# Products of probabilities and values of two attention stages, cut in quarters and placed behind the next heads' scores

## The reference

```
def gqa_attend(q, k, v, sink=None):
    ...
    s = jnp.einsum('bqhgd,bkhd->bhgqk', q.reshape(b, tq, hkv, g, d), k).astype(jnp.float32) * d ** -0.5
    ...
    o = jnp.einsum('bhgqk,bkhd->bqhgd', p.astype(v.dtype), v)
```

## Time and profile before

| | us |
|---|---|
| median of 3 runs | 4357.2 |
| lowest, highest | 4356.22, 4358.87 |
| profiled execution, its own time | 4357.44 |
| span of the profiled execution | 4355.6 |
| PE busy in the span | 3966.4 (91%) |
| DVE busy | 2239.5 (51%) |
| ACT busy | 781.6 (18%) |
| POOL busy | 1283.9 (29%) |
| mean granted TensorE clock | 0.934 of full |

### The profile page before, as it was taken

How to read it: one execution, slowest core, us unless ns; L and a number is a source line. 1 busy time by engine, 2 the same in 40 slices (tenths; PEclk the granted TensorE clock), 3 DMA queues, 4 the chain that set the end, 5 groups by cost and what they waited for, 6 DMA issues and landing times.

```text
span 4355.6 us, 45380 instructions
## 1 busy us (share of the span) xinstructions
PE 3966.4 (91%) x18926; PEld 3230.5 (74%) x18926; DVE 2239.5 (51%) x3645; ACT 781.6 (18%) x1462; POOL 1283.9 (29%) x522
## 2 busy tenths in 40 slices
PE   7976789999997889999999877999999999779998
PEld 5965459999985468888887745788788877457886
DVE  4824556876663462234347364733552473746334
ACT  3014432011122421100002222100100022221001
POOL 1310002333331034444443300444444433003443
PEclk9989899999998999999999956999999999569999
DMA  5410002344321012232222200222232222002222
GB/s 200 150 34 1 1 6 75 119 129 126 124 68 39 0 63 97 97 111 97 97 97 84 82 1 1 82 97 97 82 99 97 97 85 85 0 1 83 97 97 82
DMA packets 103695, 335.61 MB, mean 77 GB/s; under 512 B 11426, under 2 KB 11586, under 8 KB 103236
## 3 DMA queue, kind: packets, MB, share of 16 engines
q1 hardware_dynamic: 78192, 282.29, 19.4%
q10 hardware_dynamic: 25300, 50.43, 3.7%
HBM read 330.58 MB, written 2.10 MB: 76 GB/s over the span
## 4 chain that ended last, share of the span: by engine, by line
PE 59%; DVE 6%; ACT 2%; issue 1%; DVEq 0%; ACTq 0%
PE PS L497 50%; PE PS L979 1%; DVE XH L778 1%; PE PS L1861 1%; PE PS L499 0%; DVE H_r L655 0%; PE PS L1613 0%; PE PS L1614 0%; ACT arena L877 0%; PE PS L970 0%; PE PS L890 0%; PE PS L1864 0%; DVE small L1009 0%; PE PS L1631 0%; PE PS L2028 0%
## 5 line engine op out<-in xcount | busy, mean ns | idle before, releaser
L497 PE MATMUL PS<-arena_r,ring_hi 128*128 128x512 f32 (+1 forms) x6272 | 2120.4, 376 | 107.2 <-DVE H_r L655 102.3
L2220 POOL TENSOR_TENSOR ring_r<-ring,ring_hi 128x1024 fp32r<-128x1024 f32 x518 | 1283.7, 2479 | 3036.8 <-DVE ring_hi L337 3036.8
L497 PE MATMUL PS<-arena_r,ring_r 128*128 128x512 f32 (+1 forms) x4800 | 1800.9, 375 | 0.0
L497 PEld LDWEIGHTS PS<-arena_r,ring_hi 128*128 128x128 f32 x6272 | 1177.5, 189 | 291.5 <-issue 108.2
L497 PE MATMUL PS<-H_r,ring_hi 128*128 128x512 f32 (+1 forms) x3328 | 1249.9, 376 | 0.0
L497 PEld LDWEIGHTS PS<-arena_r,ring_r 128*128 128x128 f32 x4800 | 907.0, 189 | 132.9
L497 PEld LDWEIGHTS PS<-H_r,ring_hi 128*128 128x128 f32 x3328 | 632.4, 190 | 93.5 <-issue 0.5
L337 DVE CAST ring_hi<-ring 128x1024 fp32r<-128x1024 f32 x518 | 502.7, 973 | 276.1 <-DMA ring<-weights_dram 275.6
L1482 DVE SCALAR_TENSOR_TENSOR arena<-arena,PS 128x512 f32<-128x512 f32 x88 | 60.4, 687 | 447.3 <-PE PS L497 447.3
L1478 ACT ACTIVATE arena<-PS 128x512 f32<-128x512 f32 x88 | 52.6, 598 | 1073.5 <-PE PS L497 1073.5
L1093 DVE SCALAR_TENSOR_TENSOR XH<-PS,mods,XH 128x256 f32<-128x256 f32 (+1 forms) x144 | 68.5, 524 | 209.2 <-PE PS L497 209.2
(11 more groups left out here) (336 smaller groups left out, 3353.6 us busy)
## 6 DMA issues: line engine op xcount, KB each, us to landing
ring<-weights_dram SPq DMA_DIRECT2D x534, 512.0 KB, 3.3
rstd<-ada_later_dram ACTq DMA_DIRECT2D x54, 256.0 KB, 2.8
mean<-ada_later_dram ACTq DMA_DIRECT2D x53, 256.0 KB, 2.7
ada_extra<-ada_later_dram ACTq DMA_DIRECT2D x53, 256.0 KB, 2.8
XH<-xT_dram ACTq DMA_DIRECT2D x1, 3072.0 KB, 23.2
out_dram<-XH SPq DMA_DIRECT2D x8, 256.0 KB, 2.0
con<-second_dram ACTq DMA_DIRECT2D x1, 1536.0 KB
con<-first_dram ACTq DMA_DIRECT2D x1, 1280.0 KB, 7.9
```

The lines of the kernel that those rows point to most:

```text
L497: ins = pe.matmul(PS[:, o.bank, 0:hi - lo], w[:, 0, :], x, **flags)
L2220: nc.gpsimd.tensor_tensor(ring_lo[:, slot, :, :], ring[:, slot, :, :], ring_hi[:, slot, :, :].bitcast(F32), ALU.subtract).then_inc(lo_read ...
```

## The change

Only `attention` is edited, and so both stages. The block of L979 is cut in four quarters by key tiles: with 6 tiles 1, 2, 1, 2; with 5 tiles 1, 1, 1, 2; with 4 tiles one each; with 2 tiles 0, 1, 0, 1. Group g's quarters stand in steps 4g + 6 to 4g + 9, each behind that step's scores. The last group keeps its block, in the same step as before. The waits for `at_tc` and `at_oc` stand before the first quarter, and the copy-out on ACT moves from step 4g + 7 to 4g + 10. No instruction is added or taken away.

```
-                    if i >= 3 and (i - 3) % 4 == 3:
-                        gi, g = (i - 3) // 4, units[i - 3][0]
+                    if i >= 6:
+                        gi, quarter = (i - 6) // 4, (i - 6) % 4
+                        g = groups[gi]
                         kts = key_tiles(g)
-                        pe.wait_ge(at_tc.sem, at_tc.at("pe", i - 3))
-                        if gi >= 2:
-                            pe.wait_ge(at_oc.sem, at_oc.at("pe", gi - 2))
-                        for t, kt in enumerate(kts):
-                            ins = pe.matmul(PS[0:g["m"], 6 + gi % 2, :], g["v"](kt), turned[gi % 2][:, t, :],
+                        if quarter == 0:
+                            pe.wait_ge(at_tc.sem, at_tc.at("pe", 4 * gi + 3))
+                            if gi >= 2:
+                                pe.wait_ge(at_oc.sem, at_oc.at("pe", gi - 2))
+                        last = gi == len(groups) - 1
+                        for t in range(0 if last else len(kts) * quarter // 4, len(kts) if last else len(kts) * (quarter + 1) // 4):
+                            ins = pe.matmul(PS[0:g["m"], 6 + gi % 2, :], g["v"](kts[t]), turned[gi % 2][:, t, :],
                                             start=(t == 0), stop=(t == len(kts) - 1))
-                        ins.then_inc(at_o.sem, 1)
+                        if last or quarter == 3:
+                            ins.then_inc(at_o.sem, 1)
...
-                    if i >= 4 and (i - 4) % 4 == 3:
-                        gi, g = (i - 4) // 4, units[i - 4][0]
+                    if i == n + 3 or (i >= 10 and (i - 10) % 4 == 0):
+                        gi = len(groups) - 1 if i == n + 3 else (i - 10) // 4
+                        g = groups[gi]
                         act.wait_ge(at_o.sem, at_o.at("act", gi))
                         g["put"](PS[0:g["m"], 6 + gi % 2, :].rearrange("p (h q) -> p h q", h=4)).then_inc(at_oc.sem, 1)
```

## The result

Eight runs of the changed kernel gave 4310.8, 4314.9, 4315.5, 4339.1, 4339.2, 4339.6, 4340.4 and 4340.7 us: median 4339.2, against 4357.3 for the kernel before (4351.8 to 4359.4). The ratio is 0.9938, 95% interval 0.9914 to 0.9963: faster, clear of noise though by less than 1%, but not by a single amount. The times lie at **two levels** 25 us apart, and the profiled execution (4310.8) is one of the lower. Its mean granted clock is 0.935; that of the upper runs is 0.928. The forecast of 4314.3 fits the lower level, and the median lies outside the range of 4306 to 4329.

What follows compares the result with a forecast made beforehand. Bound by neither PE's work nor the DVE/ACT latency alone, paid one after the other in both attentions. Waits 21.4 + 18.7, less 2.7 block starts, plus 5.5 clock = 42.9 us: 4357.2 to 4314.3, range 4306 to 4329.

Steps and rivals of the forecast that it cites:

- The mechanism by which the waits go: Both attentions: pieces behind the scores fill the latency of DVE and ACT; 21.4 and 18.7 us gained without clock.
- The periods: Steady groups of four heads: second attention 13.1 to 13.4 us instead of 15.52, five-tile first attention 14.8 to 15.2 instead of 16.96.
- Block starts: 25 added starts in the first attention, 21 in the second: 0 to 5.4 us of cost, 2.7 taken.
- The sum: Whole kernel: 21.4 + 18.7 - 2.7 + 5.5 = 42.9 us saved.
- The tails' low clock: Ends of both attentions: low clock worth 4.8 us, half of it expected back.
- The clock does not come back: Rival: idle time in the tails keeps the clock low, so 37.4 us saved, 4319.8; chance 0.20.
- half hidden: Rival: first attention stays latency-bound in every second head, losing about half its 21.4; 4325 us, chance 0.08.
- not hidden: Rival: a quarter ends up in the latency path, groups still take 15.5 us; 4357 us, chance 0.03.
- slower: Rival: each of 46 re-entries into an accumulation costs PE a fixed time; at 1.2 us each 4367, chance 0.03.
- the first attention's account: First to last block: 153.6 us, PE work 125.0, rest 28.6, of which 25.4 go, 21.4 without clock.
- What stays of it: 1.5 from the low clock at the start of the stage: First attention's start: of the 28.6 us beyond PE work, 1.5 stays as low-clock loss (block 3.43 against 1.93).

Runs made afterwards that it cites:

- e6: Changed kernel with whole blocks in the four 2-tile groups of the first attention: 4318.8 to 4320.0 us, one run 4328.5; ratio 0.9923 to the kernel before.
- e12: e6 again, to count levels: 4318.2 to 4328.8 us, ratio 0.9921 to the kernel before.
- e7: Changed kernel with only the four 2-tile groups cut, whole blocks elsewhere in both attentions: 4348.2 to 4353.4 and 4373.4 to 4378.4 us, ratio 1.002.
- e10: e7 once more for a profile of its upper level; fell on the lower one, 4349.2 us.
- e13: e7 a third time for a profile of its upper level; fell on the lower one, 4353.8 us.
- e14: e7 repeated again for a profile; came out at the upper level, 4374.3 us.
- e2: The changed kernel with nothing edited, run for a second profile: 4341.0 us, an upper run.
- e1: The changed kernel with nothing edited, six runs: 4316.6 to 4316.9 and 4340.7 to 4341.8 us, ratio 0.9941.
- e8: Changed kernel plus three unused products of constants in the stage ahead of the first attention: 4309.0 to 4310.8 and 4328.7 to 4329.6 us, ratio 0.9919.
- e5: Changed kernel with group 0 of the first attention kept as one whole block: 4308.3 to 4313.7 and 4343.2 to 4343.5 us, ratio 0.9936.
- e11: e5 once more for a profile of its upper level: 4343.5 us.
- e4: Changed kernel with quarters in the second attention alone, whole blocks in the first: 4331.4 to 4334.4 us, ratio 0.9949.
- e9: e5 plus three unused 512-column products of constants right before its whole block: 4316.5 to 4325.0 us, ratio 0.9924.

## Why the prediction was right and where it was wrong

**The mechanism by which the waits go was right.** Pieces behind the scores lie inside the latency of DVE and ACT: PE's waits on ACT's copy went from 35.5 us to 2.3, the 2.4 on DVE are gone, and no new wait took their place. The periods were forecast at 13.1 to 13.4 and 14.8 to 15.2 us and are 12.94 and 15.20.

**Block starts.** 0 to 5.4 us were allowed for 46 more starts, 2.7 taken. The rows show both ends: 0.14 for each piece in the first attention (1.00 for a tile of 0.86), nothing in the second. That makes 25 x 0.14 = 3.5 us. I had looked for the cause in the 64-row scores of the first attention, and so read the rule of the Trainium skill ("TensorE: Matmul & The Clock Gate", on what each phase is for) that weights are loaded ahead of running products when row groups do not conflict. The rows do not bear that out: the piece at 608.84 stands behind a turning over 128 rows and costs 1.00 as well. (The upper bound of 5.4 also counted the 21 starts of the second attention, which has no 64-row scores at all.) The two attentions differ in something else too, the weights of these products (128*64 in the first, 128*128 in the second), and the cause stays open.

**The sum, at the lower level.** Forecast 42.9, measured 44.4 in the two stages. That it fits so well is in part luck, since two misses cancel: 22.3 in the first where the terms give about 24 (21.4 less 1.8 for starts, 3.1 and half of 2.4 for clock), 22.1 in the second where they give 19 (18.7 less 0.9, plus 1.2). The tails' low clock came back whole, 4.8 and not half of it, and the second attention's starts were free. In the first the starts cost 3.5 and not 1.8, and even in this profile the low clock at the start lasted longer, from 468.5 to 484.2 with PE at work where it had been 469.6 to 483.0: 2.3 us more at half speed, about 1.1 lost. "The clock does not come back", "half hidden", "not hidden" and "slower" by re-entry all fell at this level: the last blocks run at full clock, and no piece pays more than 0.14.

**The step that failed** is in the first attention's account: "What stays of it: 1.5 from the low clock at the start of the stage". I took the low start as a fixed loss of the block at 479.92 that ends by itself at 483, whatever stands there. The row 479.92 with 3.43 instead of 3.67 us showed that the clock rose *in the whole block*, and the change takes exactly that block away. 9 of 15 runs are at the upper level, and in the profile of one nothing raises the clock for another 60 us. With whole blocks in the four 2-tile groups no run of ten is there (e6, e12); with cuts in them alone 8 of 15 are (e7, e10, e13, e14). PE has no waits left there, so a halved clock is paid in full: 26.5 us in that stage, more than its 22.3 of gain. I had clock only as something that waits take away and their absence gives back; the rival that a PE without waits might stay low was missing. The sentence of the Trainium skill ("TensorE: Matmul & The Clock Gate", on what is actually happening) that activity releases the throttle pointed the same way as I did. e2's row does not agree with it: 74.7 us of work in 75.0, and the clock stayed at 1.2 GHz. The measurement decides. Where the median of a few runs falls is then a matter of the draw: 4339.2 in the first eight, 4328.8 in the six of e1, with nothing edited.

**A version without the upper level.** Whole blocks in the four 2-tile groups, quarters everywhere else (e6, e12): medians 4319.1 and 4319.8, 0.992 of the kernel before, against 0.994 for the change as made. The intervals of these ratios overlap; over all runs the mean is 4321 us in ten runs against 4330 in fifteen of the change. It gives up 7 us in the first attention (159.5 against 152.3) and so is slower than the lower level of the change. e8 reaches the same ratio (0.9919) with two levels left.

## What to carry to other kernels

When a chain of other engines sets the pace and one engine's big block stands outside it, cut the block and lay the pieces into the latency; the gain is the waits, and the sum of start-to-start durations came within 2 us of it here (42.9 against 44.4). Before cutting, look in the trace at what PE was doing each time its granted clock rose: if it was in the very block that is to be cut, at a place where the clock starts low, keep blocks whole there. One was not enough here (e5, e11), four were (e6, e12). And where a profile looks as forecast but the runs don't, look at all the runs and profile again until one of the other level is caught.

## What the runs showed that was not expected

At 1.2 GHz PE stayed without a wait for 53 to 75 us and the clock did not rise (e2, e11, e14), in stretches of 128-column turnings and 256-column scores over 64 rows with a pair of 512-column products every 5.9 to 9.9 us. In every profile the first rise of the clock behind the low start of the first attention came in or within 2 us behind products of 512 columns; the same order of instructions gave both outcomes, 6 against 9 of 15 runs. No run of the changed kernel lay between its levels, so as far as the times tell the clock rose behind the first quarter or behind none of the others in the 2-tile groups. What decides between them in a run is visible in no row and stays open. And after a rise the clock fell again with no wait longer than 0.83 us just ahead (e4, e11), and did not fall behind the same wait elsewhere (e5, e9). With whole blocks it was back within 7 us (e4), with quarters after 54.6 (e11).
